# A tile's attention, projection, queries and expert choice beside the expert gathers of the tile ahead

## What is computed

```python
z = (x * (1 + scale1) + shift1) @ w_in            # one projection, 8004 columns
oa, s_new = hgrn2_recurrence(...)                 # branch A, 8 heads, 128x128 state
score = relu(qi . kidx) weighted by wi            # branch B: 4 index heads of 64
idx = top_k(score, min(256, L // 4))              # 128 of 512 keys, 256 of 1028
ob = softmax(q . k[idx] + bias) @ v[idx]          # 8 heads, 2 key heads, 128 wide
y = (sigmoid(gate_a) * oa + sigmoid(gate_b) * ob) @ w_out
x = LN1(ALPHA * x + gate1 * y);  h2 = x * (1 + scale2) + shift2
q = h2 @ w_q                                      # PEER: 8 heads, 2 halves of 128
s1, i1 = top_k(half 1, 16);  s2, i2 = top_k(half 2, 16)
eid, g = best 16 of the 256 pairs, softmax of their sums
out = sum_e g_e * gelu(u[eid_e] . h2) * v[eid_e]  # 8 x 16 experts a token, of 16384
x = LN2(ALPHA * x + gate2 * out)
```

## Time and profile before

| | us |
|---|---|
| median of three runs (2880.85 to 2892.33) | 2891.01 |
| the profiled execution's own time | 2880.32 |
| its span | 2878.5 |

### The profile page before, as it was taken

One profiled execution on the slowest core, in us unless ns is written; L12 is line 12 of the kernel. 1 busy time (PEld: TensorE's weight loads), 2 busy tenths in 40 slices (PEclk: granted clock), 3 DMA queues, 4 the chain that ended last, 5 costly groups with the idle time before them and its releaser, 6 DMA issues. The chain is left out here.

```text
span 2878.5 us, 23028 instructions
## 1 busy us (share of the span) xinstructions
PE 1963.0 (68%) x6978; PEld 973.7 (34%) x6978; DVE 1439.8 (50%) x2969; ACT 537.1 (19%) x1735; POOL 701.5 (24%) x606
## 2 busy tenths in 40 slices
PE   7999999977776667494099654455545555555557
PEld 2388886524442346342043211111111111111111
DVE  1000000127639666346478878556665575645554
ACT  0001000013421112101022222222221222222222
POOL 0000000012200000021134444344443444444443
PEclk9999999987765868697599877777777777787879
DMA  7522121101122322422589998999999999999996
GB/s 269 208 69 78 59 88 48 47 21 40 47 63 64 104 63 74 172 100 65 193 351 411 413 421 336 380 421 421 417 395 399 421 408 418 415 421 421 421 420 284
DMA packets 184480, 709.94 MB, mean 247 GB/s; under 512 B 28995, under 2 KB 75043, under 8 KB 114580
## 3 DMA queue, kind: packets, MB, share of 16 engines
q0 software_dynamic: 78976, 572.70, 48.6%
q1 hardware_dynamic: 105382, 135.77, 14.8%
HBM read 696.95 MB, written 13.68 MB: 247 GB/s over the span
## 5 line engine op out<-in xcount | busy, mean ns | idle before, releaser
L1490 PE MATMUL PS<-uv,dg 128*32 128x512 f32 x2176 | 768.7, 785 | 548.4 <-ACT dg L1428 541.2
L1613 DVE CUSTOM_DVE_ANT_0 uv<-uv,h2r 128x1024 f32<-128x1024 f32 x512 | 627.4, 1225 | 492.5 <-DMA uv<-in_peer_uv,eidr 471.1
L1399 POOL DMA_INDIRECT uv<-in_peer_uv,eidr x512 | 577.0, 1127 | 856.1 <-PE PS L1490 677.8
L1490 PEld LDWEIGHTS PS<-uv,dg 128*32 128x32 f32 x2176 | 228.0, 129 | 1069.1 <-ACT dg L1428 829.0
L344 PE MATMUL PS<-hT,wb 128*128 128x272 f32 (+1 forms) x1696 | 390.7, 394 | 7.0 <-PEq L132 7.0
L344 PEld LDWEIGHTS PS<-hT,wb 128*128 128x128 f32 (+1 forms) x1696 | 315.0, 186 | 83.6 <-issue 8.8
L1435 ACT ACTIVATE acts<-dots 128x2 f32<-128x2 f32 x272 | 55.3, 203 | 1075.9 <-DVE dots L1613 1075.9
L1475 PE MATMUL PS<-h2T,wq 128*128 128x416 f32 x256 | 96.3, 530 | 101.8 <-DMA wq<-in_w_peer_q 101.8
L474 POOL DMA_DIRECT2D lbp<-in_lb_param x2 | 1.8, 915 | 624.4 <-POOLq L132 624.4
L1428 ACT ACTIVATE dg<-fold,wts 128x32 f32<-128x32 f32 x544 | 140.6, 305 | 0.0
L391 DVE TENSOR_TENSOR mg_s<-mg_s,sg 128x544 f32<-128x544 f32 x8 | 5.8, 725 | 238.4 <-ACT sg L376 238.4
(11 more groups left out here) (286 smaller groups left out, 1929.9 us busy)
## 6 DMA issues: line engine op xcount, KB each, us to landing
wb<-in_w_in SPq DMA_DIRECT2D x15, 2048.0 KB, 7.7
w_ada_b<-in_w_ada SPq DMA_DIRECT2D x12, 2048.0 KB, 7.9
kvr<-in_cache_k SPq DMA_DIRECT2D x64, 128.0 KB, 2.0
kvr<-in_cache_v SPq DMA_DIRECT2D x64, 128.0 KB, 2.0
wq_b<-in_w_peer_q SPq DMA_DIRECT2D x4, 2048.0 KB, 12.7
h2r<-h_d SPq DMA_DIRECT2D x16, 512.0 KB, 13.9
uv<-in_peer_uv,eidr POOLq DMA_INDIRECT x512, 14.9
wq<-in_w_peer_q SPq DMA_DIRECT2D x8, 1024.0 KB, 26.1
```

Source lines behind the costliest of these rows:

```text
L1399: nc.gpsimd.indirect_dma_start(out=uv[j % RING][:, :], out_offset=None, in_=table, in_offset=bass.IndirectOffsetOnAxis(ids, 0)).then_inc(e ...
L1490: mm = nc.tensor.matmul(PS[ST * g:ST * g + ST, at:at + 512], dg[:, j % DR, :], uv[j % RING][:, D + 512 * half:D + 512 * half + 512], start ...
L1613: c.step(nc.vector.tensor_tensor_reduce(out=uv[j % RING][:, 0:D], in0=uv[j % RING][:, 0:D], in1=h, scale=1.0, scalar=0.0, op0=ALU.mult, op ...
```

## The change

Blocks 4 to 6 become one block. A list `beats[q]`, q from -1 to 272, is filled by `put(first, per, *steps)`: step i of a group goes to beat first + int(i / per). Every engine's stream walks through the beats: the beat's expert work (VectorE its dots of beat q, ScalarE the activations and diagonals of beat q, TensorE the values of beat q - 1, GpSimd the gathers of beat q + 4, behind its steps), and its part of each step in the beat. Beat -1 holds all of tile 0: attention, projection (y), norms, flip, queries with searches and best pairs, picks, spread. Tile t + 1's steps lie in the 64 beats of tile t, partly in those before.

```diff
+    i0, s0_, y0, q0 = tile_steps(0)
+    put(-1, 1e9, *s0_, *att(0), *y0, *norms(0), ("flip", 0, 0), ("h2r", 0, 0), ("h2r", 1, 0), *q0, *picks(0), ("spread", 0, 0), ("spread", 0, 1))
+    for t, b in ((1, 0), (2, 58), (3, 121)):
+        ix, tp, ys, qs = tile_steps(t)
+        put(b, 2, *ix)
+        b1 = b + 2
+        put(b1, 3 if t == 1 else 2, *tp)
+        b2 = b1 + (6 if t == 1 else 9)
+        put(b2, 1 if t == 1 else 0.75, *att(t))
+        b3 = b2 + (7 if t == 1 else 9)
+        put(b3, 1, *ys)
+        put(b3 + 8, 1, *norms(t))
+        put(b3 + 13, 1, ("flip", t, 0))
+        put(b3 + 14, 1, *qs)
+        put(b3 + 32, 1, *picks(t))
+        put(b3 + 41, 1, ("spread", t, 0), ("spread", t, 1))
...
+    S = 175
+    put(S, 1, ("sset", 0, 0), ("sset", 1, 0))
+    put(S + 2, 2, *[("six", b, 0) for b in range(NB)])
+    put(S + 6, 1, ("smid", 0, 0), ("smid", 1, 0), ("smid", 2, 0))
+    put(S + 9, 1.5, *[("stop", r, 0) for r in range(KSEL_S // 8)])
+    put(S + 10, 0.5, *[("sk", b, 0) for b in range(NB)])
+    put(S + 31, 1, ("smask", 0, 0), ("smax", 0, 0), ("snorm", 0, 0), ("sflip", 0, 0))
+    put(S + 36, 1, *[("sv", b, 0) for b in range(NB)])
+    put(S + 45, 1, ("smerge", 0, 0))
+    put(S + 46, 2, *[("y", TILES, c) for c in range(KD)])
+    put(S + 50, 1, *norms(TILES))
+    put(S + 55, 1, ("flip", TILES, 0))
+    put(S + 56, 2, *[("query", TILES, n) for n in range(2 * PH + 2)])
+    put(S + 65, 1, ("ssearch", 0, 0), *picks(TILES))
...
+    for t in range(TILES):
+        put(GT * (t + 1) - 3, 1, ("fload", t, 0))
+        put(GT * (t + 1), 1, *[("fin", t, k) for k in range(5)])
```

With the ring of nine and everything else in memory, the weights no longer fit. w_out and w_peer_q are laid out by the host as 24 blocks of 128 x 1024 (w_oq) and stream through a ring of three (WRING = 3) once for each of the five tiles. A query is now 8 matmuls of one tile's 128 columns:

```diff
+            def chunk(i):
+                if i >= WRING:
+                    sp.wait_ge(w_use, i - WRING + 1)
+                sp.dma_start(wr[:, i % WRING, :, :], dap(a["w_oq"], (i % WCH) * P * KD * P, [[KD * P, P], [P, KD], [1, P]])).then_inc(w_in[i % WRING], 16)
...
+                sp.wait_ge(t_merge, 2 * (t + 1))
+                vectors(t)
+                for c in range(3, 11):
+                    chunk(WCH * t + c)
+                rows_out(t)
...
-                for k in range(KD):
-                    last = nc.tensor.matmul(bank(n % 2, REST), wq2[:, (n // 2) % 2, k, P * (n % 2):P * (n % 2) + P], h2T[:, k, P:N],
-                                            start=k == 0, stop=k == KD - 1)
+                    for k in range(KD):
+                        last = nc.tensor.matmul(bank(n % 2, r), wr[:, i % WRING, k, :], h2T[:, k, 0:r], start=k == 0, stop=k == KD - 1)
```

```diff
+            nc.scalar.preload_act_table_set("natural_log_exp_and_others")
```

```diff
+            sp.wait_ge(m_t5row, 2)
+            sp.dma_start(t5_d, t5row[:, :]).then_inc(m_t5out, 16)
+            sp.wait_ge(m_t5out, 16)
+            sp.dma_start(t5x_d, dap(t5_d, 0, [[0, P], [640, H], [1, 640]])).then_inc(m_t5out, 16)
             sp.wait_ge(m_row, 12)
             sp.dma_start(mod_d, modr[:, :]).then_inc(m_out, 16)
             sp.wait_ge(m_out, 16)
+            sp.wait_ge(m_t5out, 32)
```

More of the change, by code:

```diff
@@ new lines, in program, with place_of, put @@
+    s_kx = [sem(f"s_kx{i}") for i in range(2)]
+    s_kv = [sem(f"s_kv{i}") for i in range(2)]
+    s_kvu = sem("s_kvu")
+    landed = lambda j: 16 * (j // RING + 1)
+    jobs_of = lambda q: range(GROUP * q, GROUP * q + GROUP)
+    def place_of(j):
+        t, r = j // PT, j % PT
+        if t == TILES:
+            return t, r, 0
+        return t, r % (PT // 2) // 2, 2 * (r // (PT // 2)) + r % 2
+    beats = {q: [] for q in range(-1, NG + 1)}
+    def put(first, per, *steps):
+        for i, s in enumerate(steps):
+            beats[first + int(i / per)].append(s)
@@ new lines, in att, with norms, picks, tile_steps @@
+    def att(t):
+        return [("att", t, p) for p in range(7)]
+    def norms(t):
+        return [("norm", t, k) for k in range(4)]
+    def picks(t):
+        return [("pick", t, k) for k in range(9)]
+    def tile_steps(t):
+        idx = [("idx", t, h) for h in range(IH)] if t else []
+        tops = [("top", t, r) for r in range(KSEL_P // 8)] if t else []
+        return idx, tops + [("sel", t, 0)], [("y", t, c) for c in range(KD)], [("query", t, n) for n in range(2 * PH + 2)]
+    i0, s0_, y0, q0 = tile_steps(0)
@@ new lines, in pages @@
+            def pages(n):
+                for g in range(PAGES):
+                    if n < NB:
+                        src = a["cache_kt"][bass.ds(page(n, g), 1)].rearrange("o d g p -> (o d) (g p)")
+                    else:
+                        src = a["cache_v"][0, bass.ds(page(n - NB, g), 1)].rearrange("o p g d -> (o p) (g d)")
+                    sp.dma_start(kvr[:, n % 2, g, :], src).then_inc(s_kv[n % 2], 16)
+            key_pages(0)
+            key_pages(1)
+            pages(0)
@@ new lines, in _ @@
+            sp.wait_ge(s_pad, 1)
+            sp.dma_start(qipad[ID:P, :, :, :], qipad[0:ID, :, :, :]).then_inc(s_qp, 16)
+            for b in range(2, NB):
+                sp.wait_ge(s_ixm, b - 1)
+                key_pages(b)
+            sp.wait_ge(s_ixm, NB)
+            pages(1)
+            for n in range(2, 2 * NB):
+                sp.wait_ge(s_kvu, n - 1)
+                pages(n)
+            for c in range(3):
+                chunk(WCH * TILES + c)
+            sp.wait_ge(s_merge, 2)
@@ L781, in _ @@
+            vectors(TILES)
+            for c in range(3, 11):
+                chunk(WCH * TILES + c)
+            rows_out(TILES)
+            for c in range(11, WCH):
+                chunk(WCH * TILES + c)
+            sp.wait_ge(e_out, 16 * (TILES + 1))
         @block.gpsimd
         def _(pool):
-            nc.gpsimd.memset(qpad[:, :, :, :], 0.0)
-            nc.gpsimd.memset(qipad[:, :, :, :], 0.0).then_inc(t_pad0, 1)
+            c = Counts(pool, u_pch)
+            table = dap(a["peer_uv"], 0, [[2 * D, PK * PK], [1, 2 * D]])
@@ new lines, in index_keys @@
+            def index_keys(b):
+                if b == 0:
+                    pe.wait_ge(s_pad, 1)
+                    pe.wait_ge(s_qp, 16)
+                    nc.tensor.matmul(bank(2, ST), qiall[:, :], ki_s[:, SEQ:N], start=True, stop=True)
+                pe.wait_ge(s_kx[b % 2], 128 * (b // 2 + 1))
+                for half in range(2):
+                    lo = ID * half
+                    last = nc.tensor.matmul(bank(half), qipad[lo:lo + ID, b, :, :], kxc[lo:lo + ID, b % 2, :, :], start=b == 0, stop=b == NB - 1)
+                last.then_inc(s_ixm, 1)
@@ L902, in _ @@
-            weighted(len(heads) - 1)
+            last.then_inc(z_kn, 1)
+            for q in range(-1, NG + 1):
+                if q >= 1:
+                    values(q - 1)
+                for s in beats[q]:
+                    step(*s)
         @block.scalar
         def _(act):
-            for n, (t, h) in enumerate([(t, h) for t in range(1, TILES) for h in range(IH)]):
-                act.wait_ge(t_ix, n + 1)
-                if n >= IH:
-                    act.wait_ge(t_acc, n - IH + 1)
-                nc.scalar.activation(rel[:, h, 0:widths[t]], bank(n % 2, widths[t]), ACT.Relu, scale=ID ** -0.5).then_inc(t_rel, 1)
```

1558 lines of the change are left out of this document (763 added, 795 removed).

## The result

| | before | after |
|---|---|---|
| median of four runs each, us | 2887.34 | 2857.76 |
| lowest and highest, us | 2880.85, 2892.33 | 2851.29, 2867.48 |
| ratio, 95% interval | | 0.990, 0.989 to 0.992 |
| span of the profiled execution, us | 2878.5 | 2860.4 |
| first expert gather, us | 1398.7 | 1016.8 |

What follows compares the result with a forecast made beforehand. DMA bytes were taken to bound the last half, with the 558 us ahead leaving the DMA engines mostly idle. First gather at 1005 plus overlap of 1855 gave a 2860 us span, 2868 us on the median's scale; range 2770 to 2975.

Steps and rivals of the forecast that it cites:

- Stage one: Before the recurrence: the 2.6 MB bias table write moves here and the stage's barrier waits for it, +10 us (0 to 13).
- The recurrence: ScalarE's table loads of 1.28 us go, six in heads and three at the ends: -11.5 us (bounds 0 and -20).
- Tile 0 alone: From the recurrence's end to the first gather: attention, projection, norms, searches and choice of tile 0, 162 us (145 to 190).
- DMA bytes: Beside the gathers: 570.4 MB of gathers plus 83 MB and 28.3 MB of other traffic, 1670 us, times 1.02: 1704 us.
- VectorE's lumps in tiles 1 to 3, GpSimd: Beats where searches, heads and final norms exceed the DMA's pace, 46 us after ring smoothing; GpSimd's h2 products 6 us.
- page stall: Sample's key index, beats 177 to 180: SyncE's page issue at 9.5 us a sequence holds up the other engines, 46 us.
- the sample's work: Sample's beats: VectorE's search 9 us, mask and softmax 6, four searches in one beat 8: 23 us.
- start and tail: First gather to first dots 14 us and last dots to the end 16 us: 30 us.
- less lost: Rival: the ring hides the lumps, the page stall and the factor 1.02; -126 us, 2742 us; chance 0.20.
- Clock: Rival: TensorE at half clock in 72 beats with a weight block and the sample's 12 with two; +80, 2948 us; chance 0.18.
- Weights starve: Rival: beside gathers SyncE's queue gets 75 to 80 GB/s, a block needs 6.8 us; +35, 2903 us; chance 0.14.
- No overlap: Rival: engine-to-engine steps within a beat aren't covered by nine gathers; half the beats cost 1.1 us more; +150, 3018 us; chance 0.08.

Runs made afterwards that it cites:

- e1: Changed kernel with SyncE's wait for the spread bias table moved from the end of stage one to the last block: 2853.8 us, ratio 0.989.
- e9: Changed kernel with the 2.6 MB write of the spread bias table issued at the start of stage two, not the end of stage one: 2841.2 us, ratio 0.983.
- e5: Changed kernel with only half of each w_oq weight block loaded and that half read twice by the matmuls: 2806.6 us, ratio 0.973.
- e6: Changed kernel with weight blocks loaded whole but half of their projection and query matmuls left out: 2839.9 us, ratio 0.984.
- e4: Changed kernel with the sample's 192 cache pages copied from DRAM to DRAM into one row by SyncE in stage two: 2792.7 us, ratio 0.968.
- e7: Changed kernel with a tile's vectors and x spread behind weight blocks 3 to 8, not all ahead of block 3: 2862.2 us, ratio 0.992.
- e10: Changed kernel with e4 and e9 together and the sample's part of the mixes stored again in rows of 1 KB: 2786.0 us, ratio 0.963.
- e11: Changed kernel with VectorE's prep ahead of norm in the recurrence and 18 more TensorE matmuls in each head: 2864.4 us, ratio 0.992.

## Why the prediction was right, and where its terms were not

*Ahead of the gathers.* First gather at 1016.8, forecast 1005. Stage one: +12.5 for +10, within its bounds; the reason was half right. The write costs, but through mod_d, which stands behind it in the queue, not through the wait on the table (e1, e9), and 3.6 us have nothing to do with it. The recurrence: -11.5 was wrong. The last norm ended 12.4 us later than before, all of stage one's delay. The step that failed is that a load on the chain is worth its length: I had written for the second load of a head that it lies beside VectorE's scan, and did not ask the same of the first, whose time was VectorE's room for the norm. What stood next on the chain was the norm, and beside it TensorE's clock. My bound of 0 holds it, though not for the reason given with it: the loads did go. Tile 0 alone: 163 us for 162.

*Beside the gathers,* 1843.6 us for 1855:

| term | forecast | measured |
|---|---|---|
| DMA bytes | 1704 | 1717 (679 MB; forecast 681.7) |
| VectorE's lumps in tiles 1 to 3, GpSimd | 52 | none in sum: share 1.01, 1.01, 0.98; 12 in the beats with heads |
| page stall | 46 | 72 |
| the sample's work | 23 | 39 |
| start and tail | 30 | 18 behind the last dots, no loss at the start |

*Bytes* carried the sum, and e5 and e6 show for tiles 1 to 3 that it is bytes. The query beats took 6.7 to 6.8 us, a little above the 6.3 to 6.6 that I had given as a sign. *Lumps:* wrong. I had added up each beat's excess of VectorE over the DMA's pace; searches, final norms and GpSimd's products cost nothing that the share shows, and the heads 12 us where I had 26. That it is the ring of nine gathers that hides beats of 8 us among others of 5 fits, but no run had a smaller ring. It is the part of the rival "less lost" that came true. *Page stall:* the 57 us for six sequences were 58.9, as read from the earlier trace rows. The step that failed is the 7 us for 15 small loads: from 2100.4 to 2136.4 they took 36, 19 of them on mgS, so that TensorE had qipad 71 us after the end of the searches (2171.85) and not 42. I had priced an issue by its own length, and not by the rows that stand ahead of it in the queue. *Sample:* my price was VectorE's. By share and length, of the 39 us 12 are lost up to beat 219, 10 in the projection's beats up to 231, 4 in the query beats, 7 in beat 240 alone and 5 behind it. For the last three e6 shows TensorE as a cause: it gained 22 us from beat 219 on, of which 11 lie in beats 240 to 250 and the rest is within the spread of the clock. The first 12 us are open; e4, with no page reads, did not shorten the value beats.

*The rivals.* Clock: not in the 72 beats (e6), but in the sample's. Weights starve: its rate was misread, since 2.1 MB in 28.7 us are 73 GB/s and not 75 to 80, which makes 7.2 us a block; TensorE waited 59 us for blocks of the projection, and e7 halved this for no gain, so in tiles 1 to 3 it is at most 4 us. Less lost: in part. No overlap: not seen, tiles 1 to 3 keep a share of 1. That the forecast was 10 us from the median owes something to luck: the recurrence (12 too good), stall and sample (42 too good) and lumps (52 too bad) cancel, and the chance of 0.40 for it was not too low. The change's gain is itself a small difference of two big numbers: 382 us out, 364 us back.

## What to carry to other kernels

When a step is moved beside a saturated DMA, count its bytes first: they came back in full here, and uneven compute beside them cost little. Then look at the engine that issues: page reads, and loads in short rows ahead of the one that is waited for, were the dearest thing here, and putting the page reads in an idle stage was worth 65 us, more than twice the gain of the whole change. Before a few us are put down to an edit, look how much the same beats differ between kernels that do the same in them: 9 us here. A wait that goes from a chain is worth its length less what another engine did meanwhile in the shade of it.

## What the runs showed of the hardware

- Half of SyncE's 494 issues in the changed kernel took 0.34 to 0.47 us, but one took 19.25 us (mgS, in 1024 rows of 128 bytes, behind two more such loads), and one in e10 14.1 us (qipad, behind index pages in rows of 512 bytes and a key load of 1024 rows). Both stand behind a thousand and more short rows; qipad's own copy took 0.52 us to issue in the changed kernel, so the hold is not the DMA's that shows it. The same loads show both: gbt and mgt of tiles 0 and 1, 1024 rows of 512 bytes each, ahead of the gathers, were issued in 1.5 to 3.2 us; those of tiles 2 and 3, beside the gathers, took 19.2 to 22.7 us, and the weight block behind them 19.7. The windows of tiles 2 and 3 keep a share of 1.01 and 0.98 all the same.
- TensorE's granted clock can add 6 us to one head of 23 and nothing to the next with the same instructions. It fell in a stretch in which TensorE had hardly waited (e11), so filling the waits did not hold it. The sample's query beats took 61.7 to 71.0 us in nine kernels with the same work in them, at a granted clock of 0.72 to 0.60.
- Copies of pages from DRAM to DRAM, 18.9 MB, beside a projection in which TensorE is busy all the time, cost nothing (424.8 us for 424.7, at a DMA share of 0.28 for 0.16).
- A store of 216 KB issued 0.66 us behind one of 2.6 MB in SyncE's queue began to move 9 us after its issue (131.9), in e9, with the big one out of the way, 1.8 us after it.
